# Prompt attention's value products with high and low parts side by side, one key-value group at a time

## The reference

```
for each block of 128 queries:                     # "tile" t, 16 of them
    idx, valid = indexer_topk(qi, wi, ki, q_pos, 256)
    # sparse_attend, heads 4n..4n+3 use key-value head n
    logits = einsum('bqngd,bqknd->bqngk', q, k[idx]) * 64 ** -0.5, NEG where not valid
    p = softmax(logits)
    o = einsum('bqngk,bqknd->bqngd', p, v[idx])
```

## Time and profile before

| | |
|---|---|
| median of 3 runs | 3667.3 us (3661.36 to 3671.37) |
| the profiled execution | 3654.04 us, span 3652.4 us, mean granted TensorE clock 0.913 |
| TensorE, VectorE, ScalarE, GpSimd busy | 83%, 51%, 45%, 35% of the span |
| attention, tiles 0 to 3 | 877 to 972 us of the span, with decoding |
| attention, tiles 4 to 7, 8 to 11, 12 to 15 | 1363 to 1512, 1972 to 2201, 2752 to 3062 us, with feed-forward |

### The profile page before, as it was taken

One profiled execution on the slowest core, in us unless ns is written; L12 is line 12 of the kernel. 1 busy time (PEld: TensorE's weight loads), 2 busy tenths in 40 slices (PEclk: granted clock), 3 DMA queues, 4 the chain that ended last, 5 costly groups with the idle time before them and its releaser, 6 DMA issues.

```text
span 3652.4 us, 46908 instructions
## 1 busy us (share of the span) xinstructions
PE 3038.5 (83%) x15352; PEld 2401.1 (66%) x15352; DVE 1845.8 (51%) x4116; ACT 1636.4 (45%) x2873; POOL 1261.3 (35%) x1181
## 2 busy tenths in 40 slices
PE   7998545546678889997799999869999999799997
PEld 6887431224556668765577886646778888578886
DVE  4333972862357874467785332676772333521113
ACT  3322413622447745575563446746734444322222
POOL 1333621323013561252264114522672112224444
PEclk9999767877879999997899999979999999899999
DMA  4444344636336563353444213343443213544443
GB/s 150 139 145 150 87 128 123 173 117 200 111 123 244 210 229 126 137 209 119 184 177 166 88 63 121 128 177 132 168 174 107 70 61 125 190 149 151 173 150 124
DMA packets 216109, 529.45 MB, mean 145 GB/s; under 512 B 57514, under 2 KB 110828, under 8 KB 189852
## 3 DMA queue, kind: packets, MB, share of 16 engines
q1 hardware_dynamic: 204508, 503.85, 40.5%
q0 software_dynamic: 11360, 22.60, 2.0%
HBM read 399.43 MB, written 134.12 MB: 146 GB/s over the span
## 4 chain that ended last, share of the span: by engine, by line
PE 48%; DVE 12%; issue 11%; ACT 5%; DMA 4%; POOL 3%; SPq 2%; POOLq 0%; ACTq 0%; DVEq 0%
PE r L1622 16%; PE r L1654 12%; PE po L1702 4%; PE tr L1693 3%; ACT junk_a_b L1971 2%; POOL acc_b L2105 1%; PE sc L1681 1%; PE sc L1680 1%; PE sc L1670 1%; PE r L1811 1%; DVE junk_v_b L2344 1%; DVE trial_b L2296 1%; POOL hr_b L2086 1%; PE tr L1670 1%; DVE prob_b L2375 1%
## 5 line engine op out<-in xcount | busy, mean ns | idle before, releaser
L2105 POOL TENSOR_TENSOR acc_b<-acc_b,part_b 128x512 f32<-128x512 f32 x375 | 515.9, 1396 | 494.8 <-ACT part_b L1922 494.0
L1654 PE MATMUL r<-ready_b,h_b 128*128 128x512 f32 x2304 | 566.0, 401 | 44.4 <-ACT part_b L1922 40.3
L1654 PEld LDWEIGHTS r<-ready_b,h_b 128*128 128x128 f32 x2304 | 434.6, 192 | 160.4 <-ACT part_b L1922 52.6
L1622 PE MATMUL r<-x_hi_b,ready_b 128*128 128x512 f32 x1536 | 493.7, 395 | 5.4 <-DVE x_lo_b L2210 2.8
L2086 POOL TENSOR_TENSOR hr_b<-hr_b 128x512 f32<-128x512 f32 x128 | 148.3, 1159 | 777.0 <-ACT hr_b L1909 776.8
L1971 ACT ACTIVATE junk_a_b<-score_b,trial_b 128x384 int8<-128x384 f32 (+13 forms) x266 | 347.5, 1306 | 100.7 <-DVE trial_b L2296 99.5
L1622 PEld LDWEIGHTS r<-x_hi_b,ready_b 128*128 128x128 f32 x1536 | 291.1, 189 | 75.8 <-issue 10.1
L1922 ACT ACTIVATE part_b<-r 128x512 f32<-128x512 f32 x390 | 223.6, 594 | 217.2 <-PE r L1654 129.1
L1622 PE MATMUL r<-x_lo_b,ready_b 128*128 128x512 f32 x768 | 301.3, 392 | 0.0
L1702 PEld LDWEIGHTS po<-V_sb,pT_b 128*128 128x128 f32 x2176 | 286.1, 192 | 23.1 <-issue 3.1
L1998 ACT ACTIVATE pT_b<-tr 128x512 f32<-128x512 f32 (+3 forms) x320 | 168.7, 527 | 261.4 <-PE tr L1693 260.7
(11 more groups left out here) (407 smaller groups left out, 6055.2 us busy)
## 6 DMA issues: line engine op xcount, KB each, us to landing
ready_b<-ws_u SPq DMA_DIRECT2D x96, 1024.0 KB, 7.0
ready_b<-ws_d SPq DMA_DIRECT2D x96, 1024.0 KB, 5.0
ws_u<-up_b SPq DMA_DIRECT2D x32, 1024.0 KB, 9.2
ws_d<-dn_b SPq DMA_DIRECT2D x30, 1024.0 KB, 6.4
kv_b<-kv_pages POOLq DMA_DIRECT2D x128, 128.0 KB, 3.5
kv_b<-kv_pages SPq DMA_DIRECT2D x128, 128.0 KB, 3.1
raw_b<-w_out SPq DMA_DIRECT2D x64, 256.0 KB, 3.2
raw_b<-w_up SPq DMA_DIRECT2D x32, 512.0 KB, 5.5
```

The costliest lines, as they stand in the source:

```text
L1622: mm = pe.matmul(x[:], wt[:, c], y[:, k], start=k == n == 0, stop=(k, n) == (KD - 1, 2))
L1654: mm = pe.matmul(x[:], f[:, tok], w[:, col], start=c == n == 0, stop=(c, n) == (KQ - 1, 2))
L2105: pool.tensor_tensor(dst, dst, part[:, add_no[key] % 2, :], ALU.add).then_inc(add_pool, 1)
```

## The change

Values leave the projection as a high and a low part, side by side (`v2`, 128 columns per key-value head), and become the stationary operand of one float32r matmul per key block. The moving operand is the turned probabilities with their high and low parts side by side, 256 columns. PSUM then holds, on partitions, the high and the low part of the values' 64 columns, and on columns the high and low part of the probabilities. VectorE adds the two column halves (`sum_values`), and TensorE adds the two partition halves by a product with a matrix of two stacked identities, which also brings the queries back to the partitions (`fold_values`). Every head is scaled by itself (`output`).

The probabilities' low part is a new subtraction on VectorE for each bank (`low_prob`). A turn now waits for the consumer of the buffer two turns back, which is VectorE's `low_prob` for a bank, VectorE's `output` for a fold and ScalarE for a turned output.

Attention runs in eight lots, `LOTS`: four tiles by one key-value head. Only one key-value head's keys and values stand in SBUF; they are loaded anew between lots. Queries and masks are loaded per item (tile and key-value head). The masks of tiles 0 and 1, made on GpSimd, are stored once and loaded for the second key-value head. An A unit counts 0.45 now and AB 4.0; by the list the same feed-forward units stand among the attention units of each s as before (4 and 10, 7 and 12, 8 and 16).

```diff
-        R = {n: sb(n, s) for n, s in (("kiT", [P, NTOK]), ("V", [P, NT, P]), ("wi", [P, NT, NIH]))}
+        R = {n: sb(n, s) for n, s in (("kiT", [P, NTOK]), ("wi", [P, NT, NIH]))}
+        v2 = sb("v2", [P, 2, NKV, 2, HD], F32R)
...
+                    dve.tensor_copy(v2[:, s, :, 0], v).then_inc(v_hi_ok, 1)
...
+                    dve.tensor_tensor(v2[:, s, :, 1], v, v2[:, s, :, 0].bitcast(F32), ALU.subtract).then_inc(copied, 1)
...
-    n_bank = lambda s: 4 * NH * (s + 1)
-    ahead = lambda s: s + 2
+    LOTS = tuple((ts, v) for ts in ATTEND for v in range(NKV))
+    n_bank = lambda s: 4 * QPK * banks(LOTS[s][0][0])
+    ahead = lambda s: banks(LOTS[s][0][0]) + 1
+    STEPS = 7
...
-        return [(("AB", s), 8.0)] + [(("A", s, j), 0.5) for j in range(-ahead(s), n_bank(s) + 6)]
+        return [(("AB", s), 4.0)] + [(("A", s, j), 0.45) for j in range(-ahead(s), n_bank(s) + STEPS)]
...
+                def load_query(i):
+                    t, v = items[i]
+                    if i >= 2:
+                        sp.wait_ge(sc_full, end_score(i - 2) + 1)
...
+                def load_keys_of(s):
+                    ts, v = LOTS[s]
+                    n = width(ts[-1])
+                    if s:
+                        sp.wait_ge(sc_full, first_score(s))
...
+                def load_values_of(s):
+                    ts, v = LOTS[s]
+                    if s:
+                        sp.wait_ge(pT_used, first_score(s))
...
                 def turn_bank(key):
                     n = turn_no[key]
-                    wait(pe, tr_free, n - 1)
+                    if n >= 2:
+                        kind, m = turned_by[n - 2]
+                        pe.wait_ge({"p": pT_lo_ok, "f": o_ok, "o": aT_ok}[kind], m + 1)
                     return tr[n % 2]
...
                 def values(t, h, b):
-                    pe.wait_ge(tr_free, turn_no["p", t, h, b] + 1)
...
+                    pe.wait_ge(pT_lo_ok, prob_no[t, h, b] + 1)
...
-                        mm = pe.matmul(po[:, h, :], pT[:, prob_no[t, h, b] % 3, k - 4 * b, :], R["V"][:, k, n:n + HD],
+                        mm = pe.matmul(po[:, 0, :], V2[:, k, :], pT[:, prob_no[t, h, b] % 3, k - 4 * b].rearrange("p z q -> p (z q)"),
                                        start=k == 0, stop=k == t)
...
+                def fold_values(t, h):
+                    n = head_no[t, h]
+                    pe.wait_ge(vsum_ok, n + 1)
...
+                    x = turn_bank(("f", t, h))
+                    pe.matmul(x[:, 0:HD], vsum[:, n % 2, :], halves_one[:], start=True, stop=True).then_inc(tr_full, 1)
...
                     if (s, j + ahead(s)) in bank_of:
                         scores(*bank_of[s, j + ahead(s)])
+                    if head_end(s, j - 3):
+                        fold_values(*head_end(s, j - 3))
                     if (s, j - 2) in bank_of:
                         values(*bank_of[s, j - 2])
...
+                def low_prob(t, h, b):
+                    n, j = turn_no["p", t, h, b], prob_no[t, h, b]
+                    m = min(4, t + 1 - 4 * b)
+                    dve.wait_ge(pT_hi_ok, j + 1)
+                    dve.tensor_tensor(pT[:, j % 3, 0:m, 1, :], tr[n % 2][:, 0:m * P].rearrange("p (k q) -> p k q", q=P),
+                                      pT[:, j % 3, 0:m, 0, :].bitcast(F32), ALU.subtract).then_inc(pT_lo_ok, 1)
+
+                def sum_values(t, h):
+                    n = head_no[t, h]
+                    dve.wait_ge(pT_used, prob_no[t, h, banks(t) - 1] + 1)
...
+                    c.step(dve.tensor_copy(vsum[:, n % 2, :], po[:, 0, 0:P]))
+                    dve.tensor_tensor(vsum[:, n % 2, :], po[:, 0, P:2 * P], vsum[:, n % 2, :], ALU.add).then_inc(vsum_ok, 1)
+
+                def output(t, h):
+                    n, a, i = head_no[t, h], h % QPK, item_no[t, h // QPK]
+                    c.step(dve.reciprocal(rinv[:, a:a + 1], rsum[:, i % 2, a:a + 1]))
+                    dve.wait_ge(tr_full, turn_no["f", t, h] + 1)
...
+                    x = tr[turn_no["f", t, h] % 2]
+                    dve.tensor_scalar(o[:, i % 2, a, :], x[:, 0:HD], rinv[:, a:a + 1], None, ALU.mult).then_inc(o_ok, 1)
...
                 def attend_step(s, j):
+                    if (s, j - 1) in bank_of:
+                        low_prob(*bank_of[s, j - 1])
                     if (s, j + ahead(s)) in bank_of:
                         mask_scores(*bank_of[s, j + ahead(s)])
-                    if tile_at(s, j - 2) is not None:
-                        output(tile_at(s, j - 2))
+                    if head_end(s, j - 3):
+                        output(*head_end(s, j - 3))
+                    if head_end(s, j - 2):
+                        sum_values(*head_end(s, j - 2))
```

More of the change, by code:

```diff
@@ L1060, in blend @@
                     n, j = n + 1, j + 1
[L1061 to L1065 removed]
+            item_at[s, j - 1] = t, v
+    items = list(item_no)
+    first_score = lambda s: score_no[LOTS[s][0][0], QPK * LOTS[s][1], 0]
+    head_end = lambda s, j: bank_of[s, j][0:2] if (s, j) in bank_of and bank_of[s, j][2] == banks(bank_of[s, j][0]) - 1 else None
+    m, turned_by = 0, []
+    for s in range(len(LOTS)):
+        for j in range(n_bank(s) + STEPS):
             if (s, j) in bank_of:
                 turn_no["p", *bank_of[s, j]] = m
+                turned_by.append(("p", prob_no[bank_of[s, j]]))
                 m += 1
[L1069 to L1070 removed]
+            if head_end(s, j - 3):
+                turn_no["f", *head_end(s, j - 3)] = m
+                turned_by.append(("f", head_no[head_end(s, j - 3)]))
+                m += 1
+            if (s, j - 5) in item_at:
+                turn_no["o", *item_at[s, j - 5]] = m
+                turned_by.append(("o", item_no[item_at[s, j - 5]]))
                 m += 1
@@ L1073, in blend @@
     last_bank = lambda n: turn_no["p", *head_at[n], banks(head_at[n][0]) - 1]
+    end_score = lambda i: score_no[items[i][0], QPK * items[i][1] + QPK - 1, banks(items[i][0]) - 1]
+    made_here = lambda i: items[i][1] == 0 and items[i][0] < SELECT[0][0]
+    mask_no, n_mask = {}, [0, 0]
+    for i in range(len(items)):
+        if not made_here(i):
+            n_mask[i % 2] += 1
+            mask_no[i] = n_mask[i % 2]
     x2_d = nc.dram_tensor("x2_d", (NT, P, D), F32).ap()
```

264 lines of the change are left out of this document (143 added, 121 removed).

## The result

The changed kernel takes 3903.9 us (median of 4 runs, 3903.0 to 3906.3) where the kernel before takes 3664.3 (median of 4 runs of the same comparison, 3655.5 to 3671.4): a ratio of 1.0663, 95% interval 1.065 to 1.0677. It is slower by 240 us. The forecast said slower by 135 us, 3800; the time lies outside its range of 3650 to 3890, 14 us above the upper end.

The account below looks back on a forecast made before the run. TensorE bounds the kernel before; afterwards a ring of waits through VectorE. Full stretches 632 + 211 - 63 + 18 = 798 against 688 us, +110; tiles 0 to 3 +25; +135 on 3654.0 gives 3789, say 3800; range 3650 to 3890.

Parts of the forecast that it names:

- One of its signs: In the three full attention stretches (tiles 4 to 15) VectorE's busy share would be at 70% or more.
- nothing there waits for VectorE: Said of the traces before the change, as why they show neither VectorE as slower bound nor TensorE's 84 us gain.
- the ring: Attention's cycle of waits per head between TensorE and VectorE: mean 5.0, 6.65, 8.1 us in the full stretches, 632 us.
- At no cost: Values' split in the projection, shared load semaphores, kT_s elsewhere, masks through DRAM: free; uncovered 4 to 9 and some 5 us.
- the share that feed units hide: Three full stretches: feed-forward units falling where TensorE idles hide on average 1.1 us for each of 57 units, 63 us.
- the ends of lots: Extra end and start of a lot (drain, queries, keys, masks), three times 6 us: 18 us, bounds 0 and 40.
- rival 1: Feed units fill most gaps the ring leaves in the three full stretches: -13 us, 3655 us; chance 0.17.
- tiles 0 to 3, +25 us: First attention stretch, one bank per head: 137 us for 115, +22; with waits for the exponential +25, bounds 0 and +40.
- The wait of 14.5 us: TensorE's wait in tiles 0 to 3 for a query load queued behind page loads; it should go.
- Rival 2: TensorE stays the bound, low parts and per-head work never delaying a turn: 3667 - 84 = 3583 us; chance 0.07.
- Rival 3: TensorE's clock falls too, being busy about 75% of the full stretches: +30 to +60 us, 3850; chance 0.12.
- The rule weighed in the forecast: Mind PSUM pressure, as a faster array does not speed PSUM's evacuation; by it alone VectorE's sum would be slower.

Follow-up runs that it names:

- the run with three moves: Changed kernel with folds done together per tile and group, scores ahead of the turn, and the values' subtraction later in the projection: 3737.9 us, ratio 1.0202.

## Why the prediction was wrong, point by point

**The direction, the place and the mechanism were right.** TensorE waits for VectorE's low parts and sums, in the order of the queues, and not for VectorE's share of the work: the kernel is slower though TensorE has less to do. The sizes that went in were right as well: the step is 1.38 us (forecast 1.38), value products follow each other at 0.12 us in the median (forecast 0.118), a full low part takes 683 ns, the per-head operations 286 + 292 + 153 + 284 = 1015 ns (the forecast took 1.07 us with the semaphores' way). One of its signs did not come: VectorE is busy for 60, 56 and 56% of the three stretches (122.02 of 202 us, 153.97 of 276, 198.60 of 353), not for 70% or more, since the stretches grew by more than its work. And "nothing there waits for VectorE" was a little strong: the value products of the kernel before wait for it for 3.3 us in the earlier trace rows. Taking the time from one fold to the next for heads without a feed unit between, the ring is 4.63 us in tiles 4 to 7 (22 heads), 6.53 in tiles 8 to 11 (17) and 8.07 in tiles 12 to 15 (14); the forecast had 5.0, 6.65 and 8.1.

**Step that failed: "At no cost", the values' split in the projection.** It cost 18 us. The forecast priced it uncovered at 4 to 9 us, 0.25 to 0.53 us each, and named room on VectorE as the cover. The subtraction took 0.985 us, and VectorE's busy share is no cover for what stands ahead of an operation that others wait for. The runs with it left out and with it moved show both.

**Term that was mis-sized: the share that feed units hide, 63 us, and the ends of lots, 18.** From the same fold-to-fold times, a head with units takes its ring plus the units' matmuls (0.2325 us each, from the 5.56 us of 24 and the 2.80 of 12 in the earlier trace rows) less what is hidden: 4.2, 14.6 and 13.9 us hidden in the three stretches, 33 us in all. The three heads that run across from the first group to the second cost 5.3, 6.6 and 15.5 us more than that, 27 us. The ring was 17 us less than forecast (615 us for 632). 110 - 17 + 30 + 9 = 132 us of the 143; the other 11 lie at the stretches' starts and ends. Units come whole and TensorE takes them in order, which the forecast said against rival 1 and then did not hold its own figure to.

**Term that was mis-sized: tiles 0 to 3, +25 us.** With what lies ahead they cost 49. From fold to fold it is 3.6 us over 30 heads, with what decoding's matmuls add between them (forecast 3.4 for the ring alone). The term's own sum was loose: 110 us of ring and 52 of decoding's matmuls less the 40 that they cover are 122 us, not the 137 from which +22 was taken. Two things failed. The way from the first group to the second takes 26.5 us in place of 3.6: attention has nothing ready there, and 13.7 us of decoding's score matmuls (957.09 to 970.83) and a wait of 4.3 us for decoding's exponential stand in it uncovered, where the forecast had 40 us of decoding under the ring. And a new wait came that the forecast had under "At no cost". The wait of 14.5 us in the earlier trace rows, which ended at tile 1's first scores (902.77), did go, as forecast. But TensorE now waits for 12.5 us at tile 0's, up to 890.72. SP's own wait ahead of it (us, times, longest):

```profile
SPq L1613 <- POOL mk_sb L2208: 6.4, 1, 6.4
```

SP issued its last page load at 878.3 and then waited 6.4 us for the masks of tiles 0 and 1, which GpSimd began only when its own page loads were issued (880.80, with 3.53 us for the clearing alone); their stores stand ahead of the first query load in SP's queue, which was issued at 886.0. In the kernel before that load was issued at 859.9, ahead of GpSimd's masks, which wait for it. The order that the new store of the masks asks for is what the trace shows; no run moved it. These two are 23 + 12.5 us against the 24 us that the term is short, so some decoding was hidden elsewhere.

**Step that failed: the feed units between the stretches and the tail, which the forecast left at nothing, +40 us.** From the last turned bank of one stretch to the first scores of the next it is 399 to 407, 481 to 492 and 566 to 576 us in every version of the changed kernel, whatever its attention does, and 396 to 399, 467 to 469 and 554 to 556 in the three kernels that keep the order of units of the kernel before. So some 7, 17 and 14 us there come with the new order of units or with the loads per group. In the two profiles TensorE's idle time in the three gaps grows by 5, 12 and 15 us. Of this, 17 us are waits for queries just ahead of a stretch, the indexer's and attention's (13.7 us before, 30.6 after), and 12 are waits for ScalarE's `part` in the feed units (71.6 and 83.3). The records have 38 us more at the lower clock there and in the tail (347 for 309). Why queries and `part` come later was not tried and stays open.

**The rivals.** Rival 1 (units fill the gaps) fails by the 33 us above. Rival 2 (TensorE stays the bound) needs more than the loss of the ring: the run with neither low part nor fold shows that even then the exponential holds TensorE. The forecast had it "beside this ring"; once the ring is shorter it is the next one. Rival 3 (the clock) was partly true.

**The clock.** In the three full stretches the records of the changed kernel have 79 us at the lower granted level (1.2 of 2.4 GHz), those of before 12 us; in tiles 0 to 3, from first scores to last turn, 60 and 21. In the run with three moves they are 26 and 36 us. It falls where TensorE waits and comes back where the waits go, so it is in the main a consequence of the ring here, as far as these runs show; at half speed 67 us are worth at most 34 us of TensorE's work. The page "TensorE: Matmul & The Clock Gate" of the Trainium skill (section on HAM oscillation) names idle gaps between bursts as what brings the lower level; by that rule too the clock follows the waits, and the traces agree in direction, though the waits here are many and short (27 of 1.0 us in the mean before the folds of the last stretch, 1.5 the longest).

**The rule weighed in the forecast**, of the page "Trainium Kernel Development and Optimization" of the Trainium skill (section Best Practices), that TensorE tiling "speeds up compute but not PSUM evacuation", held in direction. The runs add what it leaves out: the same 320 evacuations cost 9 us in the kernel before, 44 in the changed kernel without a fold and 155 with it.

## What to carry to other kernels

When a result leaves PSUM by one more engine, follow the buffers and not the engines' shares: list what stands in each in-order queue ahead of the operation that gives a buffer back, and do it again for the next ring once this one is shorter. A small product that borrows a place in another stream's two buffers can cost five times its work; batch it, which gave 103 of the 148 us back. To give it buffers of its own is the other way; it was not tried here. And ask of each engine whether it issues first what others wait for: exchanging scores and turn was worth 80 us in the changed kernel and 32 in the kernel before.

## What the runs showed of the hardware

- The same VectorE subtraction of 128 columns, two operands in SBUF, took 985 ns beside a GpSimd operation on 320 columns (the addition L370 in 16 of the 17 tiles of the changed kernel), and 277 ns in the median where it stood later (the one that still lay beside that addition took 955). In the tile shown above it began 0.04 us after GpSimd's and ended 0.15 us after it. It works the other way too: where VectorE's sum of 640 columns began with GpSimd's addition, the sum took 0.81 us and the addition 1.55 in place of 0.88. The section "Who interferes with whom" of the page "SBUF — State Buffer" of the Trainium skill says that VectorE with two SBUF inputs contends with a GpSimd instruction that reads SBUF, and, of the ports that the two share, that whoever issues first has them for the whole instruction and the other is fully blocked. The traces agree for these two pairs. They agree less well for a third: beside GpSimd's addition of 64 columns (L371), which the profile has start 0.03 us earlier, the subtraction still took 0.28 us, and the addition 0.48 in place of 0.37; starts so close do not tell who issued first. A subtraction of 128 columns with one operand in PSUM (kl, L262) took 275 ns in the same tiles.
- On VectorE a copy of 128 columns out of PSUM, an addition of 128 with one operand there and a scaling of 64 out of PSUM cost 286, 292 and 284 ns each: half the columns were no cheaper. A scaling of 256 columns took 425 ns and a subtraction of 512 683.
